# A tenth ring place of 2 MB from a smaller descriptor scratch, in a two-block mixture-of-experts kernel

## The reference

```python
h = rms_norm(x, norm1_gain) * (1 + sc1) + sh1
proj = h @ w_in
x = x + g1 * ((sigmoid(gate_h) * y_h + sigmoid(gate_a) * y_a) @ w_out)
x = x + g2 * moe_ffn(rms_norm(x, norm2_gain) * (1 + sc2) + sh2, ...)
...
proj = rms_norm_2(x, norm_mix_g) @ w_in_2
x = x + (sigmoid(g_a) * branch_a + sigmoid(g_b) * branch_b) @ w_out_2
x = x + hierarchical_moe(rms_norm_2(x, norm_ffn_g), ...)
```

## Time and profile before

| | |
|---|---|
| median of 3 runs | 1577.63 us (1577.33 to 1578.7) |
| profiled execution, span of its instructions | 1575.5 us |
| the median above that span | 2.1 us |
| PE, DVE, ACT, POOL busy | 92%, 38%, 22%, 1% |
| DMA | 594.59 MB, mean 377 GB/s |
| first expert stage, second expert stage | about 245 to 1160 us, about 1366 to 1570 us |

### The profile page before, as it was taken

One profiled execution on the slowest core, in us unless ns is written; L12 is line 12 of the kernel. 1 busy time (PEld: TensorE's weight loads), 2 busy tenths in 40 slices (PEclk: granted clock), 3 DMA queues, 4 the chain that ended last, 5 costly groups with the idle time before them and its releaser, 6 DMA issues.

```text
span 1575.5 us, 20915 instructions
## 1 busy us (share of the span) xinstructions
PE 1455.8 (92%) x8704; PEld 758.2 (48%) x8704; DVE 602.0 (38%) x911; ACT 339.3 (22%) x391; POOL 20.8 (1%) x33
## 2 busy tenths in 40 slices
PE   5999999999999999999999999999989999997677
PEld 2878985333333333333333333333348999753343
DVE  4686683232222231322313223223257587322111
ACT  4564432010101110101101001011033474221110
POOL 2100100000000000000000000000000000000000
PEclk9999999999999999999999999999999999998899
DMA  9976599999999999999999999999985437899997
GB/s 382 366 262 265 197 357 379 428 428 428 427 429 427 428 429 427 428 428 428 427 428 429 425 429 428 428 430 427 429 331 190 169 124 295 358 421 422 422 422 315
DMA packets 76733, 594.59 MB, mean 377 GB/s; under 512 B 5354, under 2 KB 6592, under 8 KB 37252
## 3 DMA queue, kind: packets, MB, share of 16 engines
q1 hardware_dynamic: 74416, 588.25, 90.4%
q0 software_dynamic: 1728, 4.86, 1.0%
q10 hardware_dynamic: 532, 0.64, 0.1%
HBM read 592.66 MB, written 1.06 MB: 377 GB/s over the span
## 4 chain that ended last, share of the span: by engine, by line
PE 50%; DMA 42%; DVE 6%; issue 1%; ACT 1%; SPq 0%; DVEq 0%; ACTq 0%
PE PS L539 45%; DMA ring<-in_w_up 32%; DMA ring<-in_w_gate_e 7%; PE PS L708 3%; DMA ring<-in_w_ada 1%; DMA arena<-in_w_in 1%; DVE ring_r L349 1%; PE PS L732 1%; PE PS L648 0%; DVE arena L807 0%; PE PS L1456 0%; ACT ring_r L344 0%; DVE arena_r L349 0%; PE PS L568 0%; DVE arena L2010 0%
## 5 line engine op out<-in xcount | busy, mean ns | idle before, releaser
L539 PE MATMUL PS<-ring,arena 128*64 128x512 f32 x3020 | 670.8, 596 | 46.2 <-DMA ring<-in_w_up 38.5
L539 PEld LDWEIGHTS PS<-ring,arena 128*64 128x64 f32 x3020 | 209.8, 137 | 469.5 <-issue 389.1
L539 PE MATMUL PS<-arena 128*128 128x128 f32 (+12 forms) x1240 | 227.6, 441 | 4.8 <-ACT arena L535 1.4
L795 DVE TENSOR_SCALAR arena<-PS 128x512 f32<-128x512 f32 x32 | 22.1, 692 | 487.6 <-PE PS L539 487.6
L539 PE MATMUL PS<-ring_r 128*128 128x256 f32 (+1 forms) x576 | 171.4, 305 | 0.4 <-DVE ring_r L1935 0.3
L518 ACT ACTIVATE arena<-arena 128x512 f32<-128x512 f32 x32 | 20.2, 630 | 703.3 <-DVE arena L795 703.3
L539 PEld LDWEIGHTS PS<-arena 64*128 64x128 f32 (+6 forms) x1240 | 108.4, 165 | 121.8 <-issue 114.4
L539 PE MATMUL PS<-hT_r,ring_r 128*128 128x256 f32 x800 | 151.4, 285 | 1.1 <-DVE ring_r L349 1.1
L349 DVE TENSOR_TENSOR ring_r<-ring,ring_r 128x2048 fp32r<-128x2048 f32 x51 | 116.4, 2291 | 39.3 <-ACT ring_r L344 38.2
L539 PEld LDWEIGHTS PS<-hT_r,ring_r 128*128 128x128 f32 x800 | 127.4, 193 | 3.2 <-issue 2.3
L344 ACT ACTIVATE ring_r<-ring 128x2048 fp32r<-128x2048 f32 x51 | 97.2, 1911 | 103.5 <-PE PS L539 98.5
(11 more groups left out here) (374 smaller groups left out, 974.8 us busy)
## 6 DMA issues: line engine op xcount, KB each, us to landing
ring<-in_w_up SPq DMA_DIRECT2D x128, 2048.0 KB, 23.2
ring<-in_w_down SPq DMA_DIRECT2D x59, 2048.0 KB, 21.6
ring<-in_w_in SPq DMA_DIRECT2D x17, 2048.0 KB, 11.2
ring<-in_w_gate_e SPq DMA_DIRECT2D x14, 2048.0 KB, 20.9
ring<-in_w_up_e SPq DMA_DIRECT2D x14, 2048.0 KB, 19.6
ring<-in_w_down_e SPq DMA_DIRECT2D x14, 2048.0 KB, 20.2
ring<-in_w_ada SPq DMA_DIRECT2D x12, 2048.0 KB, 15.9
ring<-in_w_out SPq DMA_DIRECT2D x4, 2048.0 KB, 7.7
```

Of the source, the lines that this page charges most:

```text
L539: return nc.tensor.matmul(o, w, m, start=first, stop=last)
L795: V.tensor_scalar(glu.rearrange("p (kk b q) -> p kk b q", kk=4, b=2), hu[:, :, :, :, 0], 7.0, None, ALU.min)\
```

## The change

- POOL's descriptor scratch is 1 KB per partition. `rows` and `pos` have no space of their own any more; they lie over the arena (from the start of `kt`, 26 KB in).
- A new place `ring1` of 16 KB per partition (slot 10).
- `EARLY` gets a fifth member, expert 27, whose last down piece is loaded into `ring1` behind the projection unit ("in", 5) of dense stage 1. The branch of PE moves behind expert 27.
- In dense stage 2, quad 1's unit 4 is loaded into `ring1`, and the `modrow` piece of quad 1's unit 3 with it, behind the first four `MID` units; quad 1's unit 2 comes right behind quad 0's unit 0. In quad 2, unit 4 no longer waits for quad 1's down products.
- The low part of the second half of the merge moves from `cb` to the upper half of `h` (`merged2_low`), as `cb` lies inside `x2`.
- The mid norm row is loaded once the last expert's activation is transposed and copied (`m1_aT` at 32), not once expert 22 is done.
- Each router weight's load is cut in two halves over k, so `smalls` counts fifteen loads.

```diff
...
 small = sb("small", [P, NSMALL])
-rows = sb("rows", [66, P])
-pos = sb("pos", [66, P], I32)
 flag = sb("flag", [P, 2], I32)
 mod_rows = nc.dram_tensor("mod_rows", (3, 2 * D), F32, kind="Internal").ap()
+ring1 = sb("ring1", [P, SLOTW])
+with nc.sbuf_tensor("below", [P, A1MAP["kt"][0] * KB], F32) as below, nc.sbuf_tensor("rows", [66, P], F32) as rows, \
+        nc.sbuf_tensor("pos", [66, P], I32) as pos:
+    pass
 arena, arena_r = sb_twice("arena", [P, int(ARENA * KB)])
...
 slots = [ring4[:, i, :] for i in range(4)] + [ring2[:, i, :] for i in range(2)] \
-    + [at(M2MAP, n) for n in ("x0", "x1", "x2")] + [at(A1MAP, "gates")]
+    + [at(M2MAP, n) for n in ("x0", "x1", "x2")] + [at(A1MAP, "gates")] + [ring1[:, :]]
...
-EARLY = (7, 12, 17, 22)
+EARLY = (7, 12, 17, 22, 27)
 EARLY_UNITS = [MOE1 + 6 * e + 5 for e in EARLY[1:]]
...
 cv_low = at(A2MAP, "cb", mem=arena_r).rearrange("p (m t) -> p m t", m=4)
+merged2_low = at(A2MAP, "h", 1024, 1024, mem=arena_r).rearrange("p (k t) -> p k t", k=4)
 att_up = at(A1MAP, "attT", mem=arena_r).rearrange("p (m t) -> p m t", m=4)
...
           [(at(MMAP, "e0a"), 0, 2), (at(MMAP, "e0b"), 2, 1), (at(MMAP, "e0c"), 3, 1)], [(at(MMAP, "e1"), 0, 4)],
-          [(hT_flat, 0, 2), (modrow[:, 0:2, :].rearrange("p b n -> p (b n)"), 2, 1), (at(MMAP, "e2"), 3, 1)]]
+          [(hT_flat, 0, 2), (modrow[:, 0:2, :].rearrange("p b n -> p (b n)"), 2, 1), (at(MMAP, "e2"), 3, 1)],
+          [(ring1[:, :], 0, 4)]]
 EARLY_LOADS = sum(len(p) for p in PLACES) + 1
...
 QUAD0 = [SLOT_OF[MOE2 + i] for i in range(6)]
-QUAD1 = [6, 7, 8, None] + QUAD0[0:2]
+QUAD1 = [6, 7, 8, None, 10, QUAD0[1]]
 LATER = QUAD0[2:6] + QUAD0[0:2]
...
-    if quad_slot(q, i) is None:
-        return S("tenth"), 16 * len(TENTH)
+    if quad_slot(q, i) in (None, 10):
+        return S("tenth"), 16 * (len(TENTH) + 1)
     s_ = quad_slot(q, i)
...
 def _(sp):
+    def early_load(n, places):
+        w = moe1_src(EARLY[n], 5)
+        for a, k, rows_ in places:
+            sp.dma_start(a.rearrange("p (k n) -> p k n", n=1024), w[:, k:k + rows_, :]).then_inc(S("early"), 16)
     sp.dma_start(x[:, :, :], t["x"][0].rearrange("(t p) d -> p t d", p=P)).then_inc(S("x"), 16)
...
             unit_load(sp, u, d)
-    def early_load(n, places):
-        w = moe1_src(EARLY[n], 5)
-        for a, k, rows_ in places:
-            sp.dma_start(a.rearrange("p (k n) -> p k n", n=1024), w[:, k:k + rows_, :]).then_inc(S("early"), 16)
+        if d == ("in", 5):
+            early_load(4, PLACES[4])
...
             unit_load(sp, MID0 + n, MID[n], S("mid_again"))
+    def quad_load(q, i, at_=None):
+        s_ = quad_slot(q, i)
+        landed = S("tenth") if s_ == 10 else S(f"loaded{s_}")
+        sp.dma_start(moe2_pair(q, i), moe2_src(q if at_ is None else at_, i)).then_inc(landed, 16)
+    def tenth_load(dst, o, c):
+        n = 2048 if o == 0 else 1024
+        sp.dma_start(dst, moe2_src(1, 3)[:, o, c:c + n]).then_inc(S("tenth"), 16)
+    quad_load(1, 4)
+    tenth_load(*TENTH[2])
     for n in range(4, len(MID)):
...
         unit_load(sp, MID0 + n, MID[n])
-    def quad_load(q, i, at_=None):
-        s_ = quad_slot(q, i)
-        sp.dma_start(moe2_pair(q, i), moe2_src(q if at_ is None else at_, i)).then_inc(S(f"loaded{s_}"), 16)
...
     quad_load(1, 0)
-    for i in range(2):
-        wait(sp, unit_free(before_in_slot(MOE2 + i)))
-        quad_load(0, i)
+    wait(sp, unit_free(before_in_slot(MOE2)))
+    quad_load(0, 0)
+    quad_load(1, 2)
+    wait(sp, unit_free(before_in_slot(MOE2 + 1)))
+    quad_load(0, 1)
     sp.wait_ge(S("merged_lower"), 4)
...
         quad_load(0, i)
-    quad_load(1, 2)
     sp.wait_ge(S("logits"), 3)
-    for dst, o, c in TENTH:
-        n = 2048 if o == 0 else 1024
-        sp.dma_start(dst, moe2_src(1, 3)[:, o, c:c + n]).then_inc(S("tenth"), 16)
+    for piece in TENTH[0:2]:
+        tenth_load(*piece)
     sp.wait_ge(S("m2_flag"), 1)
     more = sp.value_load(flag[0:1, 1:2], min_val=0, max_val=SEQ)
-    for i in (4, 5):
-        sp.wait_ge(S("m2_gu_done"), 1)
-        quad_load(1, i)
+    sp.wait_ge(S("m2_gu_done"), 1)
+    quad_load(1, 5)
     for i in range(6):
...
             sp.wait_ge(S("m2_down_done"), 2)
-        else:
+        elif i == 5:
             sp.wait_ge(S("m2_down_done"), 4)
...
     small_load(sm("b_r2")[:, 4:36], bc(t["b_router_expert_2"][0]), "smalls")
-    small_load(sm("w_r1").rearrange("p (k n) -> p k n", k=KD),
-               t["w_router"][0].rearrange("(k p) n -> p k n", p=P), "smalls")
+    wr1 = sm("w_r1").rearrange("p (k n) -> p k n", k=KD)
     wr2 = sm("w_r2").rearrange("p (k n) -> p k n", k=KD)
-    small_load(wr2[:, :, 0:4], t["w_router_group_2"][0].rearrange("(k p) n -> p k n", p=P), "smalls")
-    small_load(wr2[:, :, 4:36], t["w_router_expert_2"][0].rearrange("(k p) n -> p k n", p=P), "smalls")
+    for ks in (slice(0, 4), slice(4, 8)):
+        small_load(wr1[:, ks, :], t["w_router"][0].rearrange("(k p) n -> p k n", p=P)[:, ks, :], "smalls")
+        small_load(wr2[:, ks, 0:4], t["w_router_group_2"][0].rearrange("(k p) n -> p k n", p=P)[:, ks, :], "smalls")
+        small_load(wr2[:, ks, 4:36], t["w_router_expert_2"][0].rearrange("(k p) n -> p k n", p=P)[:, ks, :], "smalls")
...
     pool.wait_ge(S("gain_free"), 2)
-    pool.wait_ge(S("m1_down_done"), 2 * EARLY[3] + 2)
+    pool.wait_ge(S("m1_aT"), NE)
     small_load(gain, bc(t["norm_mix_g_2"][0]), "gain")
...
-NSMALLS = 12 * 16
+NSMALLS = 15 * 16
 lb_rows = t["lower_bound_logits"].rearrange("l (h k) -> (l h) k", k=P)
...
-        with pe.Fori(EARLY[3] + 1, NE - 1) as e:
-            moe1_pe(pe, "m1", e, e + 1, arrival(EARLY[3] + 1, e), False, False)
+        with pe.Fori(EARLY[-1] + 1, NE - 1) as e:
+            moe1_pe(pe, "m1", e, e + 1, arrival(EARLY[-1] + 1, e), False, False)
         moe1_pe(pe, "m1", NE - 1, NE, arrival(NE - 1), False, True)
...
     for n in range(2):
-        split_tokens(r + 14 + n, (cv_low, hT_low[:, 4:8, :]), "merged_lower" if n == 0 else None)
+        split_tokens(r + 14 + n, (merged2_low, hT_low[:, 4:8, :]), "merged_lower" if n == 0 else None)
...
-    merged_low = (cv_low, hT_low[:, 4:8, :])
+    merged_low = (merged2_low, hT_low[:, 4:8, :])
...
-    nc = _bacc.Bacc("TRN2", target_bir_lowering=False, num_devices=1)
+    nc = _bacc.Bacc("TRN2", target_bir_lowering=False, num_devices=1, dynamic_dma_scratch_size=1024)
     arrays, t = {}, {}
...
```

## The result

The changed kernel takes **1589.42 us** (median of 4 runs, 1585.67 to 1592.48) against 1577.48 for the kernel before beside it (1576.13 to 1578.7): 1.0072 times, 95% interval 1.0059 to 1.0086. That is slower by 12 us. The forecast was 1581.0 us, with 1586.0 as the upper end: the sign and the mechanism came as forecast, the size of one term did not.

A forecast was written before the change was run, and what follows sets the result against it. DMA was taken to bound both expert stages, the order of PE and DVE the dense stages. Terms +14.2 - 6.3 - 4.5 = +3.4 us on 1577.6 gave 1581.0 us, range 1566.5 to 1586.0.

The forecast's parts named there:

- the serial halves: Dense stage 1: six router half loads go one after another at 5.1 us each, delaying DVE's L349 by 14.2 us.
- The 8.4 us of a whole matrix behind two others: Rival on the router half loads: round trips as long as 8.4 us, +34, some 1601 us; chance 0.06.
- The first expert stage: Expert 27's early load -4.2 and expert 22's skip made whole -2.1: -6.3 us, ends -4 and -7.
- the branch at expert 22: First expert stage: PE's 1.33 us gap entering the branch code there, with the norm row, cuts that skip's gain.
- The extra 2 MB in dense stage 1: Load behind ("in", 5) fits into a DMA hole: 0 us, 4.9 without that cover.
- The mid norm row: End of first expert stage: the later row lands at 1165.4, just in time: 0 us, ends 0 and some 2.
- Dense stage 2: Earlier loads of quad 1 are covered by slices of 190, 169 and 124 GB/s: 0 us.
- The second expert stage: 4.5 MB leave it, 11 us, but only part counts: -4.5 us, ends -2 and -11.
- One step: Second expert stage: quad 3's first two loads go out at 1408.53, as before.
- The other step: Second expert stage: with the queue nearly empty, quad 3 starts at 1420.9 instead of 1425.52, 4.5 us sooner.
- The case of serial halves: Router half loads one after another, trips of 4.5 to 6 us: chance 0.60, own range 1577.5 to 1586.
- The first rival: Half loads don't stall DVE: space returns piecewise or trips under 2.7 us; 1566.8 us; no or small stall 0.34.

The follow-up runs named there:

- scratch_only: The kernel before with the router loads cut in two and a 1 KB descriptor scratch: 1597.72 us, 1.014.
- halves_only: The kernel before with the router loads cut in two and the default scratch: 1576.87 us, 0.9996.
- scratch_2k: The kernel before with the router loads cut in two and a 2 KB descriptor scratch: 1580.74 us, 1.0025.
- no_expert27: own_sem_later without expert 27's early place: 1569.71 us, 0.9947.
- own_sem: The changed kernel with the six router half loads counted on a semaphore that only PE's router waits for: 1567.45 us, 0.9935.
- own_sem_later: own_sem with the six router half loads issued behind the first gate row's load, at 114 us: 1563.76 us, 0.9917.
- quarters: The changed kernel with router loads in quarters instead of halves, twelve loads instead of six: 1588.44 us, 1.0068.
- no_quad_place: own_sem_later with quad 1's unit 4 and the order of quad 1's and 2's loads as before: 1569.56 us, 0.9946.
- row_early: own_sem_later with the mid norm row loaded behind expert 22 as before: 1567.12 us, 0.9931.

## Why the prediction was right or wrong

**What failed** is one term: the serial halves, put at 46.3 + 6 x 5.1 = 76.9 and +14.2 us, where +21.9 was measured at L352. That seven row loads fit and two halves don't is in the sum (46.3, and six trips) as an estimate that no row of before shows: there POOL issued all twelve loads without a gap. The changed kernel's trace shows that order: seven rows, two rows and a half, then one half at a time. Both numbers in the term were too small. The first half went out at 47.50, as it took 46.45 - 40.34 = 6.1 us from the seventh row's issue to the eighth's, and not 5.1. The six trips took (84.6 - 47.5) / 6 = 6.2 us each, up to the end of DVE's wait. Together that is the 7.7 us from 76.9 to 84.6. In the trace a half lands 5.9 us (mean of six) behind its issue, and POOL's next issue follows some 0.3 us later, a piece the forecast did not have. From 47 to 90 us of the changed kernel, POOL's queue (packets, MB, share) and one kind of half (KB, median us to landing):

```profile
q0 software_dynamic: 256, 0.30, 2.6%
...
small<-in_w_router_group POOLq DMA_DIRECT2D x2, 8.0 KB, 6.2
```

The 256 packets are of eight loads, two rows and six halves, two for each engine in each load. So hg_norm_gain, with 5.1 us, was like a half by packets, as the forecast says, and still the wrong neighbour. It was also among the shortest of the row loads, most of which took 5.5 us in the trace of before. Bytes do not place the value either: the halves of 8 KB took 6.2 us, those of 64 KB 4.1 to 6.8. Why a half takes longer than a row is open; that by the diff a half is 512 runs, where a row load is 128, is a possible reason and not shown. The 8.4 us of a whole matrix behind two others was too far the other way. With hindsight, a value between the two rows, some 6.5, would have given 46.3 + 39 = 85.3 and +22.6, against +21.9 measured.

**Left out** was the granted clock while PE idles: it fell to 0.50 and was 0.50 in the window in which work starts again. From L352 to the first expert the delay grew from 21.9 to 23.3 us, but that this is the clock's price is not shown. In the changed kernel the clock is also at 0.66 from 160 to 170 us, with PE busy all the time; in scratch_only, where PE idles about as long and its clock also falls to 0.50, the delay against halves_only is 21.0 us at L349 and 21.1 at the first expert. scratch_only shows the whole price of the term with medians, 20.9 us, against the 14.2 forecast.

**The first expert stage**, -6.3 forecast. The profiled pair shows -4.7, of which expert 22's 2.2 was forecast as 2.1 and expert 27's 3.6 as 4.2; a loss of 1.1 us ahead of them is left. Five profiled executions with the old places (the kernel before, halves_only, scratch_only, scratch_2k, no_expert27) take 884.2 to 885.7 us from first expert to last; five with expert 27's (the changed kernel, own_sem, own_sem_later, quarters, no_quad_place) 878.5 to 879.8. The means are 884.8 and 879.1: **-5.7**. Right, within its ends. What the forecast put down to the branch at expert 22 does not show over three experts: no_expert27, with the branch there and the row outside the stage, takes 84.66 us for them, own_sem_later 84.73. (row_early, with expert 27's place but the norm row inside the stage, takes 880.8.)

**The extra 2 MB in dense stage 1**, 0. own_sem reaches the first expert at 265.01 us, the kernel before at 265.08; no_expert27, without that load, at 263.36, and own_sem_later, row_early and no_quad_place, with it, at 262.46, 263.30 and 263.75. Right, within 1 us.

**The mid norm row**, 0 with ends 0 and 2. Right: it landed in 6.6 us, not in the 11.6 of the earlier trace rows, although the DMA engines were full there too (share 1.04 from 1173 to 1179.6); why it was shorter is open. The risk that made it a rival was smaller than written.

**Dense stage 2**, 0: 217.1 us in both. Right.

**The second expert stage**, -4.5. The profiled pair shows -3.5. Across the runs, quad 0 to the end is 208.9 (before), 209.4 (halves_only), 210.9 (scratch_only), 211.0 (scratch_2k) and 210.7 (no_quad_place), mean 210.2; with the new place 205.4, 205.5, 206.3, 204.9, 205.2 and 205.0, mean 205.4: **-4.8**. Right. One step shows as written: SP's quad 3 gate loads go out at 1427.20 in the changed kernel, which is 1408.53 and the 18.7 by which quad 0 is later. The other step came out smaller: quad 3's gate products started 1442.64 - 1385.32 = 57.3 us behind quad 0, at PE's own pace, and 58.9 in the trace of before, so 1.6 us sooner; the up products 65.5 against 68.7, 3.2 sooner, with DMA the bound again. That -4.8 lies so close to -4.5 is in part luck. Idle DMA came near 1407 + 18.7, as the forecast had it (share 0.85 from 1425 to 1435 us), but the larger part lay behind the start of quad 0's gate products (0.60 from 1385 to 1395) and not ahead of it.

**The sum** with the terms as the medians and means have them: +20.9 - 5.7 - 4.8 = +10.4; measured +11.9.

**The chances.** The case of serial halves had 0.60 and was right; its own range ended at 1586 as its trips ended at 6 us, and they took 6.2. The first rival (1566.8) was wrong for the change but right as the account of what it would be without the stall: own_sem measured 1567.45. Its other condition, a trip of under 2.7 us, has one case in the traces, the landing in 2.4 us at a share of 0.08; in the changed kernel a half took 4.1 us at a share of 0.78, and 5.6 to 6.8 at 1.01 to 1.05.

## What to carry to other kernels

POOL's descriptor scratch can be cut for space in each partition, but then look at POOL's issues: at 1 KB they fell into groups here (seven rows, three quarters, one half), and each group cost one whole landing time, 3.9 to 8.2 us from issue to issue with SP's weight loads under way. Before cutting it, look at what waits on the last of those loads: a semaphore that counts loads of different urgency made 22 us here, and a few lines that moved the router's halves to another semaphore turned a loss of 12 us into a gain of 10. And a place that took one 2 MB load out of the first expert stage brought 4.9 us behind that expert, what its bytes cost there, and cost under 1 us in dense stage 1, where it went into a hole (a slice at 262 GB/s). In the second expert stage 4.5 MB, worth 11 us at the 421 GB/s of the earlier trace rows, brought only 4.8, as the first quads run at PE's pace (57.3 us for the first three).

## What the runs showed that was not expected

- At a gap POOL waited for the landing of **all** loads under way, not for the oldest: groups of 7, 3 and 1 with 1 KB, of 10, 3 and 2 with 2 KB, three quarters at a time.
- In the changed kernel the halves of the router's weights, of 8 or 64 KB, took 4.1 to 6.8 us from issue to landing at a DMA share of 0.78 to 1.05; one of 64 KB at a share of 0.08 took 2.4. The changed kernel's four runs went from 1585.67 to 1592.48, a spread of 6.8 us, where ten of halves_only had 3.2; that the length of the trips varies from run to run and makes this spread is likely and not shown.
- With PE idle from 72 to 85 us the granted clock fell to 0.50 and was still 0.50 from 85 to 92. Short stretches with a clock under 1.00 also stand where PE is busy all the time (0.83 from 140 to 150 us in the kernel before), and not in every kernel.
